# A parallel attention and DeltaNet block: four keys ahead of the index queries, four beside the first delta heads, logits in later rounds, projections first in a round

## What is computed

```python
h = rmsnorm(x, gain) * (1 + scale) + shift
proj = h @ w_in      # aq ak av az | iq ik iw | bq bk bv bz bbeta ba | ga gb
# branch A: 8 heads of 128, keys chosen by an index score
logits = einsum('bqhd,bsd->bqhs', rope(iq), rope(layernorm(ik))) * 64 ** -0.5
score = einsum('bqh,bqhs->bqs', iw, relu(logits)) * 8 ** -0.5     # causal, top 128 of 512
y_a = (softmax over the chosen keys @ v * silu(az)) @ w_a_out
# branch B: gated DeltaNet, 8 heads of 128, in chunks
q, k, v = silu(causal_conv4(bq, bk, bv)); q, k = l2norm(q), l2norm(k)
lower = strict_lower(beta * k @ k.T * decay)
t_mat = inverse(lower + eye)          # then a scan over the chunks
y_b = (rmsnorm(o_b) * silu(bz)) @ w_b_out
out = (sigmoid(ga) * y_a + sigmoid(gb) * y_b) @ w_o
return x + gate * rmsnorm(out, post_gain)
```

## Time and profile before

| | |
|---|---|
| median of three runs | 899.78 us |
| the profiled execution | 899.64 us, span 897.8 us |
| TensorE busy | 832.9 us, 93% |
| VectorE busy | 473.0 us |
| POOL busy | 392.6 us |
| ScalarE busy | 326.7 us |
| HBM traffic | 102 GB/s over the span |

### The profile page before, as it was taken

The page is one execution under the profiler, slowest core; times in us unless marked ns, Lnnn a source line. Parts: engine busy times, 40 slices in busy tenths (PEclk is TensorE's granted clock), DMA queues, the critical chain, the costliest instruction groups (busy, mean ns, idle before and its releaser), DMA issues.

```text
span 897.8 us, 11319 instructions
## 1 busy us (share of the span) xinstructions
PE 832.9 (93%) x4226; PEld 672.3 (75%) x4226; DVE 473.0 (53%) x907; ACT 326.7 (36%) x678; POOL 392.6 (44%) x262
## 2 busy tenths in 40 slices
PE   1978688999999989999999999999999999999996
PEld 0546565688888778888888777777777788878996
DVE  3455889826668777665666544445434433232104
ACT  2424432444352434425434344443334322212211
POOL 1123554355264434644535544354543543543542
PEclk9989889999999999999999999999999999999998
DMA  7933530533232332323221222232222245452502
GB/s 273 334 88 124 171 92 8 120 103 110 63 104 61 106 81 61 93 61 106 83 70 48 71 70 71 71 92 72 71 71 71 74 142 160 141 171 86 194 19 94
DMA packets 147345, 92.10 MB, mean 103 GB/s; under 512 B 17746, under 2 KB 140883, under 8 KB 146011
## 3 DMA queue, kind: packets, MB, share of 16 engines
q1 hardware_dynamic: 147290, 91.38, 34.9%
HBM read 84.52 MB, written 6.85 MB: 102 GB/s over the span
## 4 chain that ended last, share of the span: by engine, by line
PE 71%; DVE 18%; ACT 4%; issue 3%; DMA 2%; POOL 1%; SPq 0%; POOLq 0%; ACTq 0%; DVEq 0%
PE ps L588 15%; PE ps L590 15%; PE ps L589 15%; PE ps L629 3%; DVE yq L1552 2%; PE ps L859 2%; PE ps L907 2%; PE ps L906 2%; PE ps L905 2%; PE ps L846 2%; DVE binv L1611 2%; ACT prob L1144 2%; DVE kraw L1552 1%; DMA pos_i<-in_positions 1%; DVE prob L1721 1%
## 5 line engine op out<-in xcount | busy, mean ns | idle before, releaser
L1216 POOL TENSOR_TENSOR w_lo<-raw,w_hi 128x1024 fp32r<-128x1024 f32 (+1 forms) x109 | 263.5, 2423 | 351.5 <-ACT w_hi L926 351.4
L588 PE MATMUL ps<-h_hi,w_hi 128*128 128x512 f32 (+1 forms) x680 | 291.0, 428 | 6.0 <-ACT h_hi L948 6.0
L590 PE MATMUL ps<-h_hi,w_lo 128*128 128x512 f32 (+1 forms) x680 | 269.1, 396 | 0.0
L589 PE MATMUL ps<-h_lo,w_hi 128*128 128x512 f32 (+1 forms) x680 | 267.7, 394 | 0.0
L588 PEld LDWEIGHTS ps<-h_hi,w_hi 128*128 128x128 f32 (+1 forms) x680 | 129.8, 191 | 32.5 <-ACT h_hi L948 6.8
L590 PEld LDWEIGHTS ps<-h_hi,w_lo 128*128 128x128 f32 (+1 forms) x680 | 128.8, 189 | 29.8 <-issue 0.5
L589 PEld LDWEIGHTS ps<-h_lo,w_hi 128*128 128x128 f32 (+1 forms) x680 | 129.7, 191 | 26.1 <-issue 3.6
L926 ACT ACTIVATE w_hi<-raw 128x1024 fp32r<-128x1024 f32 (+1 forms) x109 | 113.3, 1050 | 18.2 <-PE ps L907 17.1
L1085 ACT ACTIVATE o_tok<-ps 128x128 f32<-128x128 f32 x32 | 8.9, 278 | 107.4 <-PE ps L811 107.2
L629 PE MATMUL ps<-w_ada_sb,cb 128*128 128x512 f32 x64 | 30.2, 633 | 11.5 <-DVE rp L1376 11.5
L906 PE MATMUL ps<-w_lo,y_hi 128*128 128x256 f32 x128 | 36.2, 283 | 0.0
(11 more groups left out here) (274 smaller groups left out, 1445.8 us busy)
## 6 DMA issues: line engine op xcount, KB each, us to landing
raw<-in_w_in SPq DMA_DIRECT2D x84, 512.0 KB, 3.8
w_ada_sb<-in_w_ada SPq DMA_DIRECT2D x8, 1024.0 KB, 19.5
raw<-in_w_b_out SPq DMA_DIRECT2D x8, 512.0 KB, 3.8
raw<-in_w_a_out SPq DMA_DIRECT2D x8, 512.0 KB, 4.1
ada<-in_w_ada SPq DMA_DIRECT2D x8, 512.0 KB, 4.8
raw<-in_w_o SPq DMA_DIRECT2D x8, 512.0 KB, 4.0
inverse_tiles<-zero SPq DMA_DIRECT2D x2, 1032.0 KB, 5.0
x_sb<-in_x SPq DMA_DIRECT2D x1, 2048.0 KB, 10.0
```

What stands on the lines that cost most here:

```text
L588: pe.matmul(out_ap, w_hi[:, slot, k, 0:m], rhs_hi(k), start=(k == 0), stop=False)
L589: pe.matmul(out_ap, w_hi[:, slot, k, 0:m], rhs_lo(k), start=False, stop=False)
L590: mm = pe.matmul(out_ap, w_lo[:, slot, k, 0:m], rhs_hi(k), start=False, stop=(k == KT - 1))
L1216: pool.tensor_tensor(w_lo[:, slot, :, 0:n], raw[:, slot, :, 0:n], w_hi[:, slot, :, 0:n].bitcast(F32), ALU.subtract).then_inc(lo_made, 1)
```

## The change

- The units: S and K0 to K3 come first, then I0 to I3 and GA0 to GA3. K4 and K5 follow Z of delta head 0, K6 and K7 follow Z of head 1. So heads 0 and 1 take 20 rounds each, and `R_DELTA` is 44, 64, 84, 100 and on as before. The number of units and rounds stays.
- New rounds: taps of keys 0, 4, 8, 12, 60, 64, 80, 84; grams 10, 12, 16, 19, 67, 69, 87, 90; masks 9, 10, 11, 12, 14, 15, 16, 18; inverse 23 and 96; units I0 to I3 end at rounds 16, 20, 24, 28.
- The logits get a list of their own, `R_LOGIT`: rounds 22 to 24, 27 to 29, 32 to 34, 37 to 39.
- TensorE does `part(r)` at the head of its round instead of at its end.
- The waits follow the new order: which swish, solve and z step frees a buffer for which key.

```diff
-UNITS = ([("S", 0), ("K", 0)] + [("K", h) for h in range(1, 6)] + [("I", n) for n in range(4)]
+UNITS = ([("S", 0), ("K", 0)] + [("K", h) for h in range(1, 4)] + [("I", n) for n in range(4)]
          + [("GA", n) for n in range(4)])
-for _h, _extra in enumerate((("K", 6), ("K", 7), ("GA", 4), ("GA", 5), ("GA", 6), ("GA", 7), ("AQ", 0), ("AK", 0))):
-    UNITS += [("Q", _h), ("V", _h), ("Z", _h), _extra]
+for _h, _extra in enumerate(([("K", 4), ("K", 5)], [("K", 6), ("K", 7)], [("GA", 4)], [("GA", 5)], [("GA", 6)], [("GA", 7)],
+                                [("AQ", 0)], [("AK", 0)])):
+    UNITS += [("Q", _h), ("V", _h), ("Z", _h)] + _extra
...
-R_LOW = [10, 11, 13, 14, 17, 18, 46, 50]
-R_GRAM = [13, 15, 17, 19, 22, 26, 74, 90]
-R_INV = [25, 97]
+R_LOW = [9, 10, 11, 12, 14, 15, 16, 18]
+R_GRAM = [10, 12, 16, 19, R_DELTA[1] + 3, R_DELTA[1] + 5, R_DELTA[2] + 3, R_DELTA[2] + 6]
+R_INV = [23, R_DELTA[2] + 12]
+R_LOGIT = [ends_at("I", m // 6) + 6 + m // 6 + m % 6 // 2 for m in range(24)]
...
-R_ATT = [192] + [188 + 16 * h for h in range(1, HEADS)]
+R_ATT = [R_DELTA[7] + 28] + [begins("AQ", h) + 16 for h in range(1, HEADS)]
...
             for m, (hd, qt) in enumerate(LOGITS):
-                if r != ends_at("I", hd // 2) + 4 + m % 6 // 2:
+                if r != R_LOGIT[m]:
                     continue
...
-            if h >= 6:
-                pe.wait_ge(*solve_act.at("kd", h - 5))
+            if h >= 4:
+                pe.wait_ge(*solve_act.at("kd", h // 2 - 1))
...
                 if h == 0:
-                    pe.wait_ge(*gram_dve.at("L", 5))
+                    pe.wait_ge(*gram_dve.at("L", 3))
...
                 if h in (1, 2):
-                    pe.wait_ge(*gram_dve.at("L", h + 5))
+                    pe.wait_ge(*gram_dve.at("L", 2 * h + 3))
...
         for r in range(N_ROUNDS):
+            part(r)
             for h in range(HEADS):
                 scan(h, r - R_DELTA[h])
...
                 gate_sum()
-            part(r)
...
-                if h >= 6:
-                    act.wait_ge(*z_dve.at("s", h - 6))
+                if h >= 4:
+                    act.wait_ge(*z_dve.at("s", h // 2 - 2))
...
-                act.wait_ge(*key_dve.at("s", 5 if h == 0 else 6 if h == 1 else 7))
+                act.wait_ge(*key_dve.at("s", min(2 * h + 3, HEADS - 1)))
...
-            if r == ends_at("I", 3) + 8:
+            if r == R_LOGIT[-1] + 1:
```

## The result

The changed kernel takes **901.03 us** (median of 20 runs, 899.67 to 902.48), the kernel before 899.68 beside it (20 runs). The ratio is 1.0016 with an interval of 1.0009 to 1.0023: 1.35 us slower, inside the bound of 0.2% that the prediction called no change, and inside its range of 889 to 904, but on the other side of zero from the forecast of 2.4 us less. The profiled execution took 899.69 us (span 897.9).

What follows compares the result with a forecast made beforehand. TensorE is busy 93% of the span, so only waits and clock could be won; VectorE paces the front. Front -7.2, overlaps +6.8, second inverse -2.0 gave -2.4 against 899.64: 897.3 us, range 889 to 904.

Steps and rivals of the forecast that it cites:

- L of key 0: Front, before gram 1: lower tiles ready at 102.3 us (bounds 101 and 104.5), TensorE waits 5.5 us.
- L(2): Front, before gram 3: lower tiles late, ready at 122.3 us (121 to 123.5), TensorE waits 6.8 us.
- The overlaps: Delta stage, keys 4 to 7 beside the scans: waits of 4.0 and 4.9 us against 2.1 before, 6.8 us given back.
- The second inverse: Idle time from 300 to 323 us: of 4.9 us, 2 are taken back (0 to 3).
- the front's gain: Up to head 0 of the delta stage: 188.4 against 195.6 us, 7.2 us gained (bounds 3 and 11).
- I leave 2.5 us (1 to 6): Front, logits and first inverse, rounds 23 to 31: 2.5 us lost, with about 19 us of work on VectorE and TensorE each.
- Part 3: part(r) first in every round: nothing gained, at worst 0.5 us lost at the first AO unit.
- part 1: Front: four keys ahead of the index queries, grams and masks at new rounds, part first; gives 7.2 us.
- C: Rival, gram between state and residual: price grows with each VectorE delay; 904.8 us, or 901.5 with front as summed; chance 0.20.
- D: Rival: POOL's w_lo of unit 6 holds L of key 0 to 104.5 or later; front +4, total 900.5 us; chance 0.10.
- B: Rival: overlaps hardly cost more than before, POOL's masks come in time for L(2); 889.5 to 894 us; chance 0.30.
- Case A: As summed: front +7, overlaps nearly eat it; 897.3 us, own range 894 to 901; chance 0.40.

Runs made afterwards that it cites:

- experiment 4: Changed kernel with only the masks of keys 4 to 7 moved from rounds 14 to 18 to rounds 40 to 43: 897.0 us, ratio 0.9970.
- experiment 7: Changed kernel with the first inverse in round 28 in place of 23: 896.21 us, ratio 0.9969.
- experiment 3: Kernel before with one edit, part(r) at the head of TensorE's round: 892.96 us, ratio 0.9930.
- experiment 2: Changed kernel with part(r) back at the end of the round: 906.46 us, ratio 1.0084.
- experiment 5: Changed kernel with grams 4 and 6 one round earlier (66 and 86): 898.78 us, ratio 0.9987.
- experiment 8: Changed kernel with masks 0 to 3 in rounds 10 to 13 in place of 9 to 12: 899.1 us, ratio 1.0000.
- four moves: Changed kernel with masks 0 to 3 in rounds 10 to 13, masks 4 to 7 in 40 to 43, grams 4 and 6 one round earlier, first inverse in 28: 886.89 us.
- one move and part(r) first: Kernel before with part(r) first, first inverse in round 32 instead of 25, lower-tile load of heads 4 and 5 behind it: 889.45 us, ratio 0.9892.
- experiment 1: The changed kernel once more, unedited, as base and second profile: 901.12 us, ratio 1.0018.
- experiment 12: Changed kernel with the logits at their old distance behind the index queries: 903.43 us, ratio 1.0039.

## Why the prediction was wrong

**What held.** The walk through the front was right wait by wait: round 6 about 1 us (1.17), gram 0 0.6 (0.69), L of key 0 ready at 102.3 with a wait of 5.5 (101.04, 5.26), L(2) at 122.3 with 6.8 (121.58, 6.97). The cause given for L(2), index queries on VectorE behind a copy on ScalarE behind POOL's masks, is shown by experiment 4: VectorE stood idle for 5.64 us. The overlaps were to wait 0.85 + 2.2 + 0.9 and 0.85 + 2.2 + 0.85 + 1.0, 8.9 us in all; they waited 0.78 + 1.98 + 0.52 and 0.83 + 1.96 + 0.60 + 0.81, 7.5. (For the wait of 2.2 the terms listed add to 6.4 us, not 7.5; the rest is what the words "after TensorE's group" stand for, 0.99 us of VectorE's idle time before U at 227.38 us.) L797 came to 10.5 us in sum, 10 foretold. The second inverse gave 1.5 us back for the 2 taken. Overlaps and second inverse together: +4.8 forecast, +4.2 measured. For part(r) at the end of the program nothing was forecast, and nothing is there. The mark of head 0, foretold at about 176 us, left out that quarter 44 now stands ahead of it, 1.36 us.

**The step that failed is the front's gain**, 7.2 us forecast and 3.4 measured. Of the 3.8 us missing, 2.4 are the term "I leave 2.5 us (1 to 6)" for logits and inverse: the waits alone were 4.86 us (0.79, 1.60, 0.52, 1.95). The prediction set VectorE's 19 us of work in rounds 23 to 31 against TensorE's 19 and took the small remainder. It counted neither that VectorE would stand 1.73 us for the inverse's tiles nor that two scores would take 4.43 us beside POOL's passes, where two of the same size take 1.42 us at 146.33 us in the kernel of experiment 7. The held scores alone were absorbed: with the inverse out of the way (experiment 7) they are as long, and 1.2 us of waits are left. The inverse beside scores that nothing holds was not tried. The other 1.4 us are spread over the front: the ledger allowed 4.9 us of loss outside the waits, all of it clock, and about 6.2 are there. The half clock behind the two grams is 4.1 of them, as foretold (101.04 to 105.19 and 121.58 to 125.67 us at 0.50); the 0.9 for round 6 did not come; what the remaining 2.1 are stays open. The mechanism was right and the size wrong: the measured 3.4 us lie within the term's bounds of 3 to 11, at their lower end.

**What the sum could not show.** The prediction never priced part(r) ahead of the round by itself; under "Part 3" it stands as nothing beyond the details, and its real effects are spread through part 1 (1.3 us of wait, 0.8 of clock, kx 1.5 us earlier), 3.6 us at most. Alone it is worth 6.3 us, in the new order 5.3 (experiments 3 and 2). The 2.7 us between 3.6 and 6.3 are in part clock (1.7 us rather than 0.8) and in part a chain on VectorE that comes clear of POOL (1.4 us for two products instead of 3.1); the parts were not measured one by one. Against the kernel with part(r) first alone the new order of keys, grams, masks, logits and inverse costs 8 us, where by the prediction's steps it would have cost about 1 (-2.4 + 3.6). Two errors, a gain priced too low and a loss priced too low, hid each other down to 3.7 us. That the result came so near the forecast is in this sense luck. At head 0 the new order is 1.8 us behind its own work list against experiment 3 (121.43 against 132.11 us from the first projection step, 12.5 us of work less), at head 4 6.5 us (286.50 against 280.00).

**The median.** The forecast for the profiled execution and that for the median were taken as one number, since the three runs of before lay within 0.5 us. Twenty runs spread further: 897.6 to 900.6 us before (all but the lowest from 899.0), 899.7 to 902.5 for the changed kernel. In the changed kernel waits of about 2 us were followed by half clock in one profile and not in the other, which was no term of the sum; at an equal start about 0.6 us of the median would be left to it, an estimate, since the starts of the other runs are not on record.

**The rivals.** C (the gram between state and residual) is real in its place, and experiment 5 takes its 2.3 us away; but it cost what the sum said, not the price at which C decides. D (w_lo of unit 6 in the chain of kx) held L(0) up by about 1.0 us (gram 1 stands 42.16 us behind the first projection step, 41.15 in experiment 8, where its wait is 3.85 instead of 5.26), already inside the 102.3. B fell: VectorE was late in both overlaps and POOL's masks did not come in time. Case A, whose own range ended at 901, is what happened, at its edge: its front gave 3.4 us instead of 7.

**Two small slips of the working** change nothing: L(1) is 108.4 by its own terms, not 108.7, and C with the front as summed 901.6, not 901.5.

**What stays open**: which executions get the additional half clock, where 2.1 us of the front's loss lie, and whether the new order is better by itself once both are tuned. 886.9 (four moves) against 889.5 (one move and part(r) first) suggests it, but in the old order masks and grams were left where they stood.

## What to carry to other kernels

Price each edit of a change by itself, also one that seems to be mere bookkeeping, and try it alone: here one moved line was worth 6.3 us and the planned reordering -8. When work of an engine that sets the pace is placed beside a group with a tight hand-over, count its waits and the operations of the neighbour that hold it, not only its busy time; moving the inverse five rounds gave 4.4 us without removing anything. Compare two executions from a mark ahead of the change, or the start of the run is read as an effect of the edit.

## What the runs showed of the hardware

**Short waits can cost clock, and not in each run.** The wait of 2.30 us in round 6 was followed by a stretch at 0.79 before and 0.62 in experiment 2, the wait of 1.17 us in the same place by none. Waits of 1.96 to 1.98 us were followed by 0.79 in one execution and by 1.00 in another of the same kernel (experiment 1), waits of 0.71 us in that place by none. Seven profiles here have such a wait for the third residual in both overlaps (the changed kernel twice, and experiments 2, 4, 7, 8 and 12): of these 14 waits 6 were followed by a stretch below full clock, both in experiments 4 and 12, one each in the second profile and in experiment 2, none in the other three. A stretch at 0.79 over 8 us cost 0.9 us (head 2 to head 3, experiment 1) to about 1.7 us (experiment 3).

**A tiny operation can be held as long as a large one.** In VectorE's and POOL's timelines of the changed kernel, L1589 works on 128 x 4 numbers and takes 0.17 us in gram 3; in gram 2 it took 2.10 us and ended 0.04 us behind POOL's w_lo. The sum over 128 x 512 numbers just ahead of it took 0.69 us:

```profile
117.04 0.69 DVE L1587 TENSOR_REDUCE kst<-diag 128x4 f32<-128x512 f32 x1
117.76 2.10 DVE L1589 TENSOR_SCALAR kst<-kst 128x4 f32<-128x4 f32 x1
...
125.11 0.17 DVE L1589 TENSOR_SCALAR kst<-kst 128x4 f32<-128x4 f32 x1
```

```profile
115.75 1.78 POOL L1259 TENSOR_TENSOR iq<-iq,tab_cos 128x512 f32<-128x512 f32 x1 [1.38 <-DVE isw L1506]
117.49 2.33 POOL L1218 TENSOR_TENSOR w_lo<-raw,w_hi 128x1024 fp32r<-128x1024 f32 x1
```

The Trainium skill (SBUF — State Buffer, Who interferes with whom) says that VectorE's tensor_scalar can enter a mode that takes both port pairs, when its operands meet the conditions of that mode, and that the engine that issues first keeps the shared pair for its whole instruction. By that rule, this row agrees: POOL's w_lo had begun 0.27 us earlier. The same section of the Trainium skill says that a tensor_reduce never contends on this chip. The trace agrees: each of the eight reductions of the grams (L1587) took 0.69 us, the one at 117.04 us too, with POOL's two passes beside it.
